# Per-head means of an fp32 decoder trunk: fp32 products replaced by products of rounded high and low parts, three stages moved

## The reference

```python
# retention head
mu = o_ret.mean(-1, keepdims=True)
var = jnp.mean(jnp.square(o_ret - mu), -1, keepdims=True)
o_ret = (o_ret - mu) * lax.rsqrt(var + LN_EPS)
o_ret = o_ret... * jax.nn.silu(rg)
# HGRN2 head
o_h = o_h * lax.rsqrt(jnp.mean(jnp.square(o_h), -1, keepdims=True) + LN_EPS) * p['hgrn_norm_w']
o_h = o_h... * jax.nn.silu(hg)
mixed = jnp.concatenate([o_ret, o_h], axis=-1)
return mixed @ p['w_out_ab'], ...
```

## Time and profile before

| | us |
|---|---|
| median of 3 runs (1495.84, 1500.84, 1495.93) | 1495.93 |
| the profiled execution, its own time | 1500.38 |
| the profiled execution, span from first to last instruction | 1498.6 |
| PE busy | 1438.2 (96%) |
| DVE busy | 850.0 (57%) |
| ACT busy | 624.1 (42%) |
| POOL busy | 60.9 (4%) |
| mean granted TensorE clock | 0.985 |

### The profile page before, as it was taken

One profiled execution on the slowest core, in us unless ns is written; L12 is line 12 of the kernel. 1 busy time (PEld: TensorE's weight loads), 2 busy tenths in 40 slices (PEclk: granted clock), 3 DMA queues, 4 the chain that ended last, 5 costly groups with the idle time before them and its releaser, 6 DMA issues.

```text
span 1498.6 us, 24285 instructions
## 1 busy us (share of the span) xinstructions
PE 1438.2 (96%) x10240; PEld 1404.0 (94%) x10240; DVE 850.0 (57%) x1290; ACT 624.1 (42%) x1018; POOL 60.9 (4%) x80
## 2 busy tenths in 40 slices
PE   6999999999899999999999899998999999999993
PEld 6999999989799999999999799897999999999993
DVE  4666665646755544552455787867555345424556
ACT  4343535443644313431343666726433134313434
POOL 0010101000300000000000300003000000000000
PEclk9999999999999999999999999999999999999997
DMA  7132222324132222222222122221322222222222
GB/s 260 57 98 75 74 86 76 97 83 155 43 95 75 76 94 72 84 85 85 71 78 78 44 84 72 69 71 42 99 73 85 83 76 80 85 85 74 75 64 80
DMA packets 37085, 125.22 MB, mean 84 GB/s; under 512 B 4208, under 2 KB 6384, under 8 KB 36720
## 3 DMA queue, kind: packets, MB, share of 16 engines
q1 hardware_dynamic: 33264, 112.32, 23.6%
q0 software_dynamic: 2560, 8.91, 2.1%
q10 hardware_dynamic: 1152, 2.43, 0.5%
HBM read 115.95 MB, written 7.70 MB: 83 GB/s over the span
## 4 chain that ended last, share of the span: by engine, by line
PE 90%; DVE 4%; ACT 4%; DMA 1%; issue 1%; SPq 0%; POOL 0%; ACTq 0%; DVEq 0%
PE PS L486 28%; PE PS L487 27%; PE PS L488 27%; PE PS L713 1%; DMA C<-consts 1%; ACT Y L877 1%; PE PS L628 1%; PE PS L637 1%; ACT xhi L879 1%; PE PS L643 1%; PE PS L587 1%; DVE Y L1311 1%; PE PS L608 1%; DVE Y L1308 1%; PE PS L675 1%
## 5 line engine op out<-in xcount | busy, mean ns | idle before, releaser
L486 PE MATMUL PS<-xhi,whi 128*128 128x296 f32 x2176 | 669.6, 308 | 21.8 <-DVE wlo L1070 6.9
L487 PE MATMUL PS<-xlo,whi 128*128 128x296 f32 x2176 | 656.9, 302 | 0.0
L488 PE MATMUL PS<-xhi,wlo 128*128 128x296 f32 x2176 | 654.0, 301 | 0.0
L486 PEld LDWEIGHTS PS<-xhi,whi 128*128 128x128 f32 x2176 | 414.4, 190 | 34.1 <-POOL xlo L478 14.6
L487 PEld LDWEIGHTS PS<-xlo,whi 128*128 128x128 f32 x2176 | 414.8, 191 | 1.2 <-issue 0.2
L488 PEld LDWEIGHTS PS<-xhi,wlo 128*128 128x128 f32 x2176 | 413.9, 190 | 0.0
L486 PE MATMUL PS<-hhi,whi 128*128 128x296 f32 x960 | 288.9, 301 | 4.2 <-ACT S L1015 3.1
L487 PE MATMUL PS<-hlo,whi 128*128 128x296 f32 x960 | 288.6, 301 | 0.0
L488 PE MATMUL PS<-hhi,wlo 128*128 128x296 f32 x960 | 287.4, 299 | 0.0
L744 ACT ACTIVATE whi<-raw 128x1024 fp32r<-128x1024 f32 (+1 forms) x198 | 206.9, 1045 | 179.2 <-PE PS L488 165.9
L1063 DVE TENSOR_TENSOR wlo<-raw,whi 128x1024 fp32r<-128x1024 f32 (+1 forms) x198 | 237.9, 1204 | 62.8 <-ACT whi L744 58.9
(11 more groups left out here) (208 smaller groups left out, 1122.5 us busy)
## 6 DMA issues: line engine op xcount, KB each, us to landing
raw<-weights SPq DMA_DIRECT2D x182, 512.0 KB, 3.5
raw<-weights SPq DMA_DIRECT2D x16, 384.0 KB, 3.0
Y<-xP SPq DMA_DIRECT2D x8, 296.0 KB, 9.3
Y<-xT ACTq DMA_DIRECT2D x8, 296.0 KB, 4.0
yT<-Y SPq DMA_DIRECT2D x16, 148.0 KB, 1.8
C<-consts SPq DMA_DIRECT2D x1, 2146.5 KB, 15.9
S<-s_hgrn POOLq DMA_DIRECT2D x4, 512.0 KB, 4.6
S<-s_ret POOLq DMA_DIRECT2D x4, 512.0 KB, 5.8
```

Source lines behind the costliest of these rows:

```text
L486: pe.matmul(dst, wh, h, start=first, stop=False)
L487: pe.matmul(dst, wh, lo, start=False, stop=False)
L488: return pe.matmul(dst, wl, h, start=False, stop=last)
```

## The change

The means of all heads but the last (n < LAST = 7) are no longer taken by fp32 products of the row. ScalarE rounds the row (the output for an R head's mean, the squares for a moment) into `hhi[:, n, :]`, GpSimd subtracts to get the low part into `hlo[:, n, :]`, and TensorE multiplies both parts, as fp32r, by a rounded copy `mean_r` of the matrix, adding them up in PSUM: four fp32r matmuls in place of two fp32 ones. `mean_r` is made by one ScalarE copy after the copies out of PSUM of units 0 and 1, and TensorE waits for it before unit 2. An H head's "moment" goes from 17 to 20 slots after the end; an R head's "mean" from 1 to 3, "moment" from 3 to 8, "norm" from 5 to 12, and "steps" now stands ahead of "moment". The last head keeps its code and places.

```diff
-            + [("keys", 9), ("states", 12), ("output", 14), ("sample", 17), ("moment", 17), ("steps", 18), ("norm", 27)])
+            + [("keys", 9), ("states", 12), ("output", 14), ("sample", 17), ("moment", 20), ("steps", 18), ("norm", 27)])
 R_STAGES = [...
-            ("output", -1), ("sample", 1), ("mean", 1), ("moment", 3), ("steps", 3), ("norm", 5)]
+            ("output", -1), ("sample", 1), ("mean", 3), ("steps", 3), ("moment", 8), ("norm", 12)]
+LAST = 2 * HEADS - 1
...
+        mean_r = sb("mean_r", [P, P], F32R)
...
@@ GpSimd
+            def low_part(n, i, row):
+                pool.wait_ge(part_hi, moment_count(n) + i + 1)
+                pool.tensor_tensor(hlo[:, n, :], row, hhi[:, n, :].bitcast(F32), ALU.subtract).then_inc(part_lo, 1)
             for n in range(2 * HEADS):
                 if is_h(n) and n + 2 < 2 * HEADS:
                     pool.wait_ge(o_ps, n + 1)
                     clear_scores()
+                if is_h(n):
+                    low_part(n, 0, s(HSQ))
+                elif n < LAST:
+                    low_part(n, 0, s(RO))
+                    low_part(n, 1, s(RSQ))
                 store_states(n)
@@ TensorE
+            def mean_of_parts(n, i):
+                pe.wait_ge(part_lo, moment_count(n) + i + 1)
+                for half in range(2):
+                    for part in (hhi, hlo):
+                        mm = pe.matmul(PS[:, 4 + half, 0:HT], mean_r[:], part[:, n, span(half)],
+                                       start=part is hhi, stop=part is hlo)
+                mm.then_inc(st_ps, 1)
...
+                    elif name in ("mean", "moment") and n < LAST:
+                        mean_of_parts(n, 1 if name == "moment" and not is_h(n) else 0)
...
             gemm(0, xhi, xlo, x_lo, 0, both=True, side=head_side)
             pe.wait_ge(loaded, 48)
+            pe.wait_ge(mean_rounded, 1)
             for u in range(2, U_OUTAB):
@@ ScalarE, output(n)
                 if is_h(n):
                     done(act.activation(s(HSQ), OT[:, 0:T], ACT.Square), o_sq)
+                if n < LAST:
+                    act.activation(hhi[:, n, :], s(HSQ if is_h(n) else RO), ACT.Copy).then_inc(part_hi, 1)
             def centred(n):
                 act.wait_ge(cen, n // 2 + 1)
                 done(act.activation(s(RSQ), s(RO), ACT.Square), o_sq)
+                if n < LAST:
+                    act.activation(hhi[:, n, :], s(RSQ), ACT.Copy).then_inc(part_hi, 1)
...
             evac_head(0, 0)
             evac_head(0, 1)
+            act.activation(mean_r[:], const("mean_h"), ACT.Copy).then_inc(mean_rounded, 1)
```

More of the change, by code:

```diff
@@ L308, in trunk @@
             sem("o_rstd_ready"), sem("o_mixed"), sem("mixed_hi"), sem("mixed_lo"))
+        mean_rounded, part_hi, part_lo = sem("mean_rounded"), sem("moment_rows_hi"), sem("moment_rows_lo")
         u_sb, conv, gel, hmul, h_hi, h_lo = (sem("u_in_sbuf"), sem("conv_done"), sem("gelu_done"), sem("h_ready"),
```

## The result

The changed kernel takes 1502.99 us (median of 18 executions, 1499.31 to 1509.77), the kernel before 1498.93 on the same chips (18 executions, 1495.01 to 1502.86). The ratio is **1.0033, with a 95% interval of 1.002 to 1.0046**: slower by a third of a percent, 4 to 5 us, where 1.3 us less was forecast. The forecast was 1494.6 with a range up to 1500.5, so the time is 8.4 us over it. Of these, 3.0 come from the starting point: the kernel before was put at 1495.93, the median of three executions, and is at 1498.93 in eighteen. The other 5.4 are the change's, 4.1 slower instead of 1.3 faster.

A forecast was written before the change was run, and what follows sets the result against it. TensorE, busy 96% of the span, was taken to bound the kernel. Work removed (-4.4 - 0.7), the start (+0.5) and the late norm (+3.3) gave -1.3 us: 1495.9 to 1494.6 us, range 1490.5 to 1500.5.

The forecast's parts named there:

- The TensorE work removed: TensorE, heads 0 to 6: ten means at 0.55 instead of 0.99 us, -4.4, and -0.7 at R moments, together -5.1.
- the lone moments' extra: R heads' moments standing alone took 1.22 us, 0.23 over the 0.99; losing that wait saves 3 x 0.23 = 0.7 us.
- The late norm: Diagonals after heads 1, 3 and 5: later norm delays VectorE's "begin"; TensorE waits 1.1 us each, +3.3 us.
- the chain: Fourteen pieces from TensorE's end of unit 8 (103.57) through root, norm and "begin" to a possible diagonal at 115.9.
- R heads' scores and transposed keys: TensorE's waits for H sample states before R scores, and for `rstd` before next head's keys: put at nothing.
- GpSimd: Its subtraction of 592 columns takes 1.5 us (ends 0.82 and 1.65), ready before TensorE's moment; collision with VectorE's steps: chance 0.1.
- The rule of the Trainium skill: VectorE instructions with two SBUF inputs and GpSimd instructions reading SBUF exclude each other; state steps wouldn't collide, weights' low part only past 104.3.
- The start: TensorE begins unit 2 1.0 us later, waiting for unit 1's copy and mean_r; partly at half clock, taken as +0.5 us.
- The added passes: ScalarE's ten new copies at 0.70 us each and GpSimd's subtractions at 1.5: nothing, up to 0.3 x 4 as bad end.
- The clock's rival: Half clock follows the 1.1 us waits at three diagonals, costing 3 x 1.7 = 5.1 us more: 1499.7 us; chance 0.15.
- The sum: Whole kernel: -4.4 - 0.7 + 0.5 + 3.3 = -1.3 us, from 1495.9 to 1494.6 us.

The follow-up runs named there:

- e1: The changed kernel with the R heads' norm two slots later (12 becomes 14): 1500.88 us, ratio 1.0001 to the kernel before.
- e10: e7 with TensorE's wait for mean_r moved from unit 2's start to the first mean: 1494.94 us, ratio 0.9968 to the kernel before.
- e7: The changed kernel with sixteen one-element ScalarE copies behind its copy to mean_r: 1496.05 us, ratio 0.9979 to the kernel before.
- e6: The kernel before with only eleven one-element ScalarE copies added, behind units 0 and 1's copies out of PSUM: 1501.55 us, ratio 1.0028.
- e2: The changed kernel with ScalarE's three loads of x rows issued behind the last head's value copies: 1497.42 us, ratio 0.998 to the kernel before.
- a0: The changed kernel run again, unaltered: 1502.92 us against 1500.29 for the kernel before, ratio 1.0027.
- e9: e7 with the R heads' norm at 14: 1494.15 us, ratio 0.9967 to the kernel before.
- e8: The changed kernel's stage places with the earlier fp32 products, no rounded parts, added copies, subtraction or mean_r: 1498.05 us, ratio 0.9993 to the kernel before.
- e12: The kernel before with only twenty-seven one-element ScalarE copies added: 1499.23 us, ratio 1.0001.

## Why the prediction was wrong

- **The TensorE work removed** (-5.1): right. A mean costs 0.55 in place of 0.99 at all ten places, and the lone moments' extra is gone but for 0.05: 5.0 in all, by the distances between the unit matmuls around each. e1's trace, without the diagonals' waits, shows the same: 4.5 us less over three periods and 0.4 more up to the scores of head 7.
- **The late norm** (+3.3): right in its mechanism, its place and nearly its size, 3 x 0.96 = 2.9. Each intermediate time of the chain came within 0.25 us. (Two of them are added up slightly wrong: from the terms as they stand the weights' rounding ends at 105.50, not 105.53, and the norm starts at 108.4, not 108.45; 108.35 was measured.)
- **R heads' scores and transposed keys** (nothing): the scores' burst takes 0.02 to 0.05 us more, 0.17 over four heads, and the keys' no more than before.
- **GpSimd** (1.5 us a pass, in time, no collision with the state steps): right, 1.44. The rule of the Trainium skill cited there (SBUF - State Buffer, "Who interferes with whom") is not contradicted: the second subtraction ran beside instructions with one operand in PSUM at its usual length and was through before the weights' low part at 104.35. A collision was not made.
- **The start** (+0.5): TensorE started unit 2 at 31.9 to 32.6 in the six profiles with the wait there, and at 30.3 to 31.6 in the eight without, 1.1 later on average where 1.0 was said. What it costs lies between 0.3 (e10's first diagonal against e7's) and the whole 1.1; not settled.
- **What failed is a step that was never costed.** "The added passes" priced the new ScalarE instructions by their 0.70 us and by who waits for them, and the section on the change says that the last head keeps its code and places. It does keep its code, but its place in ScalarE's instruction stream moved by seven records, which brought a fetch of instructions onto the first of three DMA issues that stand before work that TensorE waits for. The sum has no term for it. The runs show 2.3 us more of TensorE's wait (3.79 for 1.49) and +3.3 us in the profile from the scores to the end of the states, the clock's part included; e6 makes the loss without the change, and e7 takes it away with the change in place.
- **The clock's rival** was given 0.15 and tied to the diagonals. There it does not happen: neither profile of the changed kernel has half clock behind those waits of 0.7 us. It happens around the last head's wait: the stretch from there to the layer norm is 1.4 to 2.1 us longer by it in six of the fourteen profiles, the kernel before's among them, 4.5 in e2's and 7.5 in e1's long one, and not at all in six. The rival had the size of one fall (1.7) right and its place wrong.
- **The sum.** -5.0 + 2.9 + 0.2 + 0.7 (the middle of the start's) + 3.3 + 0.6 (the profiles' difference up to the layer norm) = +2.7, and 11 of 29 executions some 7 more. Measured are +4.1 (first result) and +2.6 (a0) between the medians, and 4.9 and 4.0 by the ratios. Without the fetch's 3.3 and 0.6 the same terms give -1.2, and e7 measures some -3. Its profile reaches the layer norm 3.2 us earlier than the kernel before's, and 1.5 of that is half clock behind the last head's wait, which it doesn't have; whether the change or chance keeps the clock up there is open.

## What to carry to other kernels

A change that adds instructions to an engine's queue also shifts everything behind them against the points where the engine fetches its code; where a DMA issue on a compute engine stands ahead of work that the critical engine waits for, put it behind that work, or the kernel's time hangs on the count of instructions. Before a difference of some tenths of a percent is put down to a change, pad the same queue by a handful of idle instructions in the kernel before: if that alone makes the difference, it isn't the change's. And when an engine's work is taken away, look for the queue order one engine over: here the products' gain of 5 us came with a loss of 2.9 at the diagonals, 1.8 of it from the moved stages alone and 1.1 from TensorE's earlier arrival, and moving one stage by two slots gave it back.

## What the runs showed of the hardware

- GpSimd's two-input subtraction: 0.82 us at 296 columns and 1.44 at 592, which makes an estimate of 2.1 ns a column and 0.2 us fixed.
- Waits of TensorE of 0.7 us before the diagonals were not followed by half clock. The wait of 1.5 us on the last head's values was in some profiles and not in others (the kernel before and e9 have half clock behind it, e7, e8 and e10 have none, and e12 has it only 9 us later), and waits of 2.4 us and more at this place were in all four profiles that have them. e2 has half clock there without such a wait, so the wait alone doesn't decide.
